# Attention item 0 ahead of two modulation steps, S5's angles six tiles later, constants behind the opening's last row

## The reference

```
proj = (h @ w_in).astype(f32)
m_qk, m_v, m_o, m_i, m_f, s_u, n_q, n_kv, n_g = jnp.split(proj, offs, axis=-1)
y_m = mlstm_group(...)      # 4 heads of 128, chunked over 128 tokens
y_s = s5_group(s_u, ...)    # complex diagonal state space, 32 groups of 16 channels, 64 states
y_n = nsa_group(...)        # 8 query heads, compressed, selected and windowed attention
```

## Time and profile before

| | |
|---|---|
| median of 3 runs | 2417.62 us (2417.16 to 2422.07) |
| profiled execution | 2417.42 us, its span 2415.5 us, granted clock 0.993 |
| TensorE busy | 2348.9 us, 97% |
| VectorE busy | 1861.1 us, 77% |
| ScalarE busy | 1291.3 us, 53% |
| GpSimd busy | 227.4 us, 9% |
| chain that ended last | PE 78%, DVE 14%, DMA 3%, ACT 3%, issue 2% |
| read from memory | 626.68 MB, 266 GB/s over the span |

### The profile page before, as it was taken

The page is one execution under the profiler, slowest core; times in us unless marked ns, Lnnn a source line. Parts: engine busy times, 40 slices in busy tenths (PEclk is TensorE's granted clock), DMA queues, the critical chain, the costliest instruction groups (busy, mean ns, idle before and its releaser), DMA issues.

```text
span 2415.5 us, 40088 instructions
## 1 busy us (share of the span) xinstructions
PE 2348.9 (97%) x13932; PEld 2053.2 (85%) x13932; DVE 1861.1 (77%) x2739; ACT 1291.3 (53%) x2164; POOL 227.4 (9%) x384
## 2 busy tenths in 40 slices
PE   6899999999999999999999999999999999999998
PEld 4689988788888888888889999877888888888887
DVE  7989998879999999666679987567896666665555
ACT  5365665555545545444468757655554554554444
POOL 1111111101111111000001130000110000000000
PEclk8999999999999999999999999999999999999999
DMA  9999788859999999788856865456795555555554
GB/s 379 403 391 346 276 284 304 322 196 347 341 350 341 342 341 343 238 293 271 279 205 219 312 249 169 172 184 254 296 331 191 187 187 190 189 187 205 195 193 146
DMA packets 189211, 643.06 MB, mean 266 GB/s; under 512 B 19089, under 2 KB 41809, under 8 KB 183329
## 3 DMA queue, kind: packets, MB, share of 16 engines
q1 hardware_dynamic: 125346, 421.72, 48.4%
q0 software_dynamic: 51264, 205.04, 24.1%
q10 hardware_dynamic: 12480, 14.72, 1.7%
HBM read 626.68 MB, written 14.71 MB: 266 GB/s over the span
## 4 chain that ended last, share of the span: by engine, by line
PE 78%; DVE 14%; DMA 3%; ACT 3%; issue 2%; POOL 0%; ACTq 0%; DVEq 0%; POOLq 0%
PE ps L1381 25%; PE ps L850 18%; PE ps L1389 13%; PE ps L833 9%; PE ps L1278 4%; DVE w_lo L2050 3%; DVE ada_w L2056 3%; DVE mix L2050 2%; DMA ada_w<-ada_d 2%; PE ps L818 2%; DMA ada_lo<-ada_d 1%; DVE side L2050 1%; ACT w_hi L1462 1%; PE ps L1292 1%; DVE mix L2056 1%
## 5 line engine op out<-in xcount | busy, mean ns | idle before, releaser
L2050 DVE TENSOR_TENSOR w_lo<-ring,w_hi 128x1024 fp32r<-128x1024 f32 x708 | 869.2, 1233 | 424.8 <-ACT w_hi L1462 421.1
L1462 ACT ACTIVATE w_hi<-ring 128x1024 fp32r<-128x1024 f32 x708 | 750.0, 1060 | 776.9 <-PE ps L850 244.9
L1381 PE MATMUL ps<-hT,w_hi 128*128 128x512 f32 x2688 | 642.2, 391 | 0.0
L1381 PEld LDWEIGHTS ps<-hT,w_hi 128*128 128x128 f32 x2688 | 493.9, 188 | 95.7
L2056 DVE SCALAR_TENSOR_TENSOR ada_w<-ada_w,cs_row 128x1024 f32<-128x1024 f32 (+1 forms) x332 | 406.7, 1260 | 14.5 <-DMA ada_w<-ada_d 14.2
L833 PE MATMUL ps<-hT,w_hi 128*128 128x256 f32 x2176 | 406.5, 289 | 5.5 <-DVE w_lo L2050 3.5
L833 PEld LDWEIGHTS ps<-hT,w_hi 128*128 128x128 f32 x2176 | 342.5, 193 | 16.1 <-issue 13.6
L1389 PEld LDWEIGHTS ps<-hT,w_lo 128*128 128x128 f32 x2688 | 344.6, 191 | 13.1
L1389 PE MATMUL ps<-hT,w_lo 128*128 128x256 f32 x2688 | 348.7, 283 | 0.0
L833 PE MATMUL ps<-hT,w_lo 128*128 128x256 f32 x1088 | 309.3, 284 | 0.0
L833 PEld LDWEIGHTS ps<-hT,w_lo 128*128 128x128 f32 x1088 | 210.1, 193 | 0.0
(11 more groups left out here) (327 smaller groups left out, 2356.0 us busy)
## 6 DMA issues: line engine op xcount, KB each, us to landing
ring<-stream SPq DMA_DIRECT2D x746, 512.0 KB, 4.8
ada_w<-ada_d POOLq DMA_DIRECT2D x320, 512.0 KB, 6.4
ada_w<-ada_d POOLq DMA_DIRECT2D x12, 1024.0 KB, 12.7
ada_lo<-ada_d POOLq DMA_DIRECT2D x10, 1024.0 KB, 15.7
ada_hi<-ada_d POOLq DMA_DIRECT2D x10, 1024.0 KB, 13.2
mix<-stream SPq DMA_DIRECT2D x14, 512.0 KB, 14.1
xs<-x SPq DMA_DIRECT2D x2, 2048.0 KB, 10.5
s_in_w<-mix ACTq DMA_DIRECT2D x8, 512.0 KB, 6.7
```

What stands on the lines that cost most here:

```text
L1381: m = pe.matmul(ps[:, bank, :], w_hi[:, (c + half) % SPLIT, kk * P:(kk + 1) * P], hT[:, k, :, :], start=k == 0, stop=k == KT - 1)
L1462: s.activation(w_hi[:, c % SPLIT, :], ring[:, at % RING, :], ACT.Copy).then_inc(hi_ready, 1)
L2050: return v.tensor_tensor(o, a, b, op)
```

## The change

Three edits. In layer 0 two modulation steps go from tile 26 to tiles 36 and 37, and at tile 27 the step that stood before `weighted(0)` stands behind it. The rest of the constants is loaded behind the last row of the opening, and TensorE waits for it before its first whole mixer tile. In layer 1 `s5_phases` is at tile 14 instead of 8, `s5_phases_cos` at 17 instead of 11, and the two sines of ScalarE at 18 instead of 12.

```diff
@@ -173,8 +173,8 @@
 U_DOWN, N_DOWN = (18, None), (2, 0)
 
 
-ADA_TILE = ({11: 3, 12: 3, 13: 3, 14: 1, 15: 1, 16: 1, 17: 2, 18: 2, 19: 2, 20: 2, 21: 2, 22: 1, 23: 2, 24: 1, 25: 1, 26: 3,
-             27: 2, 28: 3, 29: 1, 30: 3, 31: 3, 32: 3, 33: 6, 34: 4, 35: 5, 36: 4, 37: 3, 38: 2, 39: 3},
+ADA_TILE = ({11: 3, 12: 3, 13: 3, 14: 1, 15: 1, 16: 1, 17: 2, 18: 2, 19: 2, 20: 2, 21: 2, 22: 1, 23: 2, 24: 1, 25: 1, 26: 1,
+             27: 2, 28: 3, 29: 1, 30: 3, 31: 3, 32: 3, 33: 6, 34: 4, 35: 5, 36: 5, 37: 4, 38: 2, 39: 3},
             {0: 2, 15: 1, 16: 1, 18: 2, 19: 1, 26: 4, 28: 1, 32: 1, 33: 3})
 ADA_PIECE = ([1] * 24, [0] * 6 + [1] * 16)
 
@@ -722,8 +722,7 @@
                 pool.dma_start(head_slot(n), ada_rows[head_group(n), :, :]).then_inc(head_full[n % HEAD_SLOTS], 16)
                 if n == 1:
                     pool.dma_start(aux[:, GAINS:], aux_d[0, :, GAINS:]).then_inc(aux_in, 16)
-                if n == HEAD_SLOTS - 1:
-                    pool.dma_start(cst[:, K_FIRST:], consts[:, K_FIRST:]).then_inc(cst_rest, 16)
+            pool.dma_start(cst[:, K_FIRST:], consts[:, K_FIRST:]).then_inc(cst_rest, 16)
             for l in range(DEPTH):
                 rc = rope_c[:, :].unsqueeze(1).to_broadcast([P, 2, SEQ])
                 rs = rope_s[:, :].unsqueeze(1).to_broadcast([P, 2, SEQ])
@@ -925,7 +924,6 @@
 
                 def s5_b_transposes():
 
-                    pe.wait_ge(cst_rest, 16)
                     pe.wait_ge(aux_in, l * 16 + 16)
                     for part, name in ((0, "s_b_re"), (1, "s_b_im")):
                         for ut in range(UT):
@@ -1190,6 +1188,7 @@
                         if k in HEAD_OWN:
                             s5_own_weights(HEAD_OWN.index(k))
                     s5_in_weights(len(HEAD_IN))
+                    pe.wait_ge(cst_rest, 16)
                 for n in range(0 if l else HT, NT):
                     if l == 0 and n < HT + 2:
                         in_ev.wait(pe, l, 2 * (n - HT) + 2)
@@ -1868,7 +1867,7 @@
                             own_weights(len(HEAD_OWN) + LATE_C.index(n - 3))
                     if 0 <= n - BLOCKS_AT[l] < 2:
                         blocks(n - BLOCKS_AT[l])
-                    if n == (S5_B[1] + 3 if l else HT + 6):
+                    if n == (S5_B[3] + 3 if l else HT + 6):
                         tables(0)
                         tables(1)
                     for i in range(2):
@@ -2551,7 +2550,8 @@
                         glu_z.wait(v, l, 4)
                         glu_y.by(tt(mix[:, T_U:T_U + 4, :], mix[:, T_U:T_U + 4, :], glu_z_t, ALU.mult))
                     if 0 <= k - ITEM_TILE < NI:
-                        mixer_ada(min(ada_share(l, k - 1) + (2 if k in (GT_SLOT, GT_SLOT + 2) else 1), ada_share(l, k)))
+                        if k > ITEM_TILE:
+                            mixer_ada(min(ada_share(l, k - 1) + (2 if k in (GT_SLOT, GT_SLOT + 2) else 1), ada_share(l, k)))
                         weighted(k - ITEM_TILE)
                     mixer_ada(ada_share(l, k))
                     if l:
@@ -2571,9 +2571,9 @@
                             s5_weights_c(S5_B.index(k - 1))
                     elif k in LATE_C:
                         s5_weights_c(len(HEAD_OWN) + LATE_C.index(k))
-                    if k == (S5_B[0] + 2 if l else HT + 4):
+                    if k == (S5_B[2] + 2 if l else HT + 4):
                         s5_phases()
-                    if k == (S5_B[1] + 2 if l else HT + 5):
+                    if k == (S5_B[3] + 2 if l else HT + 5):
                         s5_phases_cos()
                     if k == ITEM_TILE + 2:
                         gate_chain()
```

## The result

The changed kernel takes 2421.72 us in the median of 22 runs (2417.64 to 2429.98), the kernel before 2419.01 us in the median of as many (2416.93 to 2422.07). The ratio over all these runs (it is not that of the two medians) is 1.0014, 95% interval 1.0008 to 1.0021: slower by 0.14%, under the 0.2% at which I would have called it slower, and not the 0.2% faster that I forecast. Its runs also scatter more upward: six of the 22 lie from 2427.07 to 2429.98 us. The profiled execution took 2419.80 us (span 2418.0).

A forecast was written before the change was run, and what follows sets the result against it. TensorE, busy 97% of the span, with VectorE as the bound from 259 us until 323.62. The terms +0.1 - 1.1 - 4.1 = -5.1 us took 2417.42 to 2412.3 us, range 2408.8 to 2418.2.

The forecast's parts named there:

- Part C: Layer 1, S5's phases, cosines and sines moved later: wait at tile 11 and half clock behind it go, -4.1 us.
- the step that failed: ScalarE near 1384 us: sines in front of a w_hi that TensorE needs some 8 us later; 0.2 us for small slips.
- The steps of C before it: Layer 1: tile 11 gains 4.3 us, phases take 3.75 us, tile 17's w_lo is ready with 2 us slack.
- GpSimd's next rotary multiplication: Before at 1350 to 1355 us: phases cheap or dear by whether it has ended; drawn out again, 3.15 us more.
- Rival (3): Slower: wait over 2.5 us at tile 17 or 18 plus half clock, 4.3 us; 2420.4 us, chance 0.14 with other losses.
- Part A: Layer 0, modulation steps moved from ahead of attention item 0 to tiles 36 and 37: +0.1 us in all.
- The first half: Attention item 0: TensorE's 2.83 us wait and half clock go, but VectorE bounds, so 2.29 us gained at 370 us.
- The term "+0.1 us" for the whole: Layer 0 modulation steps: 2.29 us gained, then paid back by item 11; bounds -2.3 and +4.1 us.
- the price of the two added steps: Tiles 36 and 37: 1.14 us each plus 0.2 us waiting for a chunk, taking -2.29 to +0.1 us.
- come two steps later in the same slots: Tiles 31 to 35: steps waiting for chunks move along with the relief, so 2.29 us gain remains at 370 us.
- Part B: Opening, constants behind the last modulation row: opening ends 1.7 us sooner, 0.6 us given back, -1.1 us.
- for a loss the moved bytes would have to cost more later: Opening's constants: no loss expected because DMA engines were full there; bounds -1.7 and 0 us.

The follow-up runs named there:

- sine_split: Changed kernel with the first of ScalarE's two sines moved from tile 18 to 17 in layer 1; 2423.59 us, ratio 1.0020 to the kernel before.
- nine: Kernel before with only S5's phases in layer 1 moved, from tile 8 to tile 9; 2418.42 us, ratio 0.9998.
- c_alone: Kernel before with only the layer 1 edit: phases at tile 14, cosines at 17, sines at 18; 2421.36 us, ratio 1.0012.
- a_late: Kernel before with only the modulation-step edit, its two added steps at tiles 38 and 39 instead of 36 and 37; 2420.73 us, ratio 1.0008.
- split_steps: Changed kernel with one sine at tile 17 instead of 18 and tile 18's two modulation steps at tile 21; 2415.74 us, ratio 0.9987 to the kernel before.
- a_alone: Kernel before with only the modulation-step edit of layer 0, including the step behind weighted(0); 2420.97 us, ratio 1.0010.
- bc_fixed: Kernel before with the constants edit and the layer 1 edit, one sine at tile 17, tile 18's modulation steps at 21; 2413.70 us, ratio 0.9989.
- steps_later: Changed kernel with tile 18's two modulation steps of layer 1 at tile 21, both sines still at 18; 2427.64 us, ratio 1.0035 to the kernel before.
- b_alone: Kernel before with only the constants loaded behind the opening's last row and TensorE's wait for them moved; 2419.48 us, ratio 1.0012.
- after: The changed kernel itself, all three edits against the kernel before; median 2421.72 us, ratio 1.0014, profiled execution 2419.80 us.
- c_fixed: Kernel before with only the layer 1 edit, one sine at tile 17 and tile 18's two modulation steps at 21; 2414.57 us, ratio 0.9984.
- b_look1: b_alone unchanged, profiled once more; 2416.57 us, first full mixer tile at 146.9 us.

## Why the prediction was wrong

**Part C, the step that failed.** "ScalarE loses one table load, 1.28 us, and has the two sines now in front of a `w_hi` near 1384; TensorE needs that chunk some 8 us later [...]" TensorE does not need the chunk at once, but VectorE's queue does (it came at 1388.82, not 1384): behind that `w_lo` stands S5's scan, and TensorE waits for the scan to have read its accumulators, not for the weights. Before the change this had 0.87 us of slack, and TensorE was to come 3 to 4 us sooner. With it the step cost 5.9 us, the wait of 2.55 and the half clock behind it, where the prediction had 0. I named what is queued behind the waiting instruction on ScalarE, and stopped there. The steps of C before it were right: 4.1 us at tile 11, `w_lo` of tile 17 in time, the phases at 3.75 us.

**The second chain.** I weighed GpSimd's next rotary multiplication only against the phases. The cosines at tile 17 stand in front of the modulation steps of tile 18, their chunk issues on POOL and the rotary multiplications behind them, and kept all of these at their old times; part C does not move one instruction on POOL's queue. The rule that I cited from the Trainium skill, "SBUF — State Buffer", section "Who interferes with whom" (an exclusive lock for a whole instruction) fits `sine_split`, with two `w_lo` in 5.9 us, and `nine`, with four in 6.8 us. GpSimd's third multiplication there fits it too: it takes 2.17 us, to 1.2 us behind the end of the first `w_lo`, where one that meets nothing takes 1.30.

**Rival (3) named the direction and nearly the size, not the place.** It has a wait of over 2.5 us at tile 17 or 18 and a fallen clock, 4.3 us. It came between tiles 20 and 21: 5.9 us in the changed kernel, 7.1 in `c_alone`. Its condition, a slip of tile 17's `w_lo`, did not occur.

**Part A.** The first half was right: TensorE is 2.3 us sooner at item 4, the wait at item 0 is gone, and the half clock behind it too, in this execution. (Of the six traces with that wait gone, `a_late` and `split_steps` have a half clock of 3.4 us some 10 us further on, behind a wait of 0.7 to 0.8 us.) The term "+0.1 us" for the whole was +1.0 in `a_alone` and +1.4 in the changed kernel, and more beside traces without A, which make up 0.2 to 1.0 us between 275 and 400 us by themselves: against `c_alone` it is 1.9 us in `a_alone`. Mis-sized was first the price of the two added steps. TensorE loses 3.3 us from 379 to 397 us in `a_alone` and 3.0 in the changed kernel, where the sum has 2.4 (from -2.29 to +0.1); of the difference 0.5 us is the chunk of tile 36, waited for 0.65 to 0.73 us instead of 0.2. The sentence that all chunks "come two steps later in the same slots" held in some executions alone: just ahead of item 10 the gain was 2.3 us in `a_alone` and 2.8 in `a_late`, but 1.6 in the changed kernel, whose wait for a chunk at 346.72 had grown from 2.33 to 3.50 us. Up to tile 36 these three have the same order in this part, so that this growth belongs to the change is not shown.

**Part B.** -1.1 us was forecast; at 275 us, ahead of part A, TensorE is 0.4 to 1.5 us ahead in four of the six traces in which the opening went its usual way, and 0.6 and 0.7 us behind in the other two (`bc_fixed`, with a half clock at 206 us, and `steps_later`). The median of `b_alone` shows no gain. What I had excluded ("for a loss the moved bytes would have to cost more later") happens by another way: in part of the executions the opening ends 5 to 7 us later than before. That two queues pace each other there was in the trace, as waits of POOL for chunks of SP's, and I used only the mean rate.

**The sum.** With the terms of the two traces: A +1.4, B -1.5, C -4.1 + 5.9 = +1.8, and +1.0 for the half clock at 1247: +2.7 us, near the +2.5 us at which the traces end. The terms are read from the same traces, so this shows that none is missing, not that each would be the same in another execution. The forecast had -5.1; C accounts for 5.9 us of the difference. The 95% interval of the ratio, +1.9 to +5.1 us, holds the sum; B's late openings come on top. Taken by themselves the three parts measured +0.10, +0.12 and +0.12%, together 0.34%, where the whole has 0.14%. With intervals of 0.09% on either side of each, no run shows whether the parts don't add or the numbers scatter. The profile that I added to, 2417.42 us, also lay 1.6 us under the median of the 22 runs.

Left open: why B's opening goes one of two ways (no run changed the order of SP's and POOL's transfers against each other), why the clock falls behind the same wait in one execution and not in another, and how much of A's extra waits is the place and how much the landing time of single chunks.

## What to carry to other kernels

When work is moved onto a queue, follow the queue behind it to its end on each engine: the instruction that is delayed may be needed late, and the one behind it at once. Slack that the move needs should be read as the smallest gap in the stretch between the operation that frees or fills a buffer and the one that waits for it, here 0.87 us. Where two chains end within a microsecond of each other, taking away one shows nothing; try both before either is called innocent. And when a median moves against the profile, look at the single runs: two groups ask for a profile of each.

## What was not expected of the hardware

- A GpSimd multiplication over 128x512 (1.30 us when it meets no VectorE operation) costs the VectorE operations beside it about as much again: a `w_lo` of 1.14 us took 2.32 us beside one and 3.68 us beside two (`sine_split`). The multiplication itself takes up to 2.3 us when the VectorE operation is ahead of it.
- Every new wait of TensorE of 1.9 us or more in the mixers (`after`, `c_alone`, `sine_split`, `steps_later`, `nine`) was followed by a stretch at the lower clock, 3.4 to 10.2 us long, and its length differed between executions of nearly the same wait. Beyond the wait itself TensorE lost 1.5 us by it in `nine`, 3.3 us in three of the others and 4.7 us in `c_alone`.
- An old wait is not always followed by one. TensorE waits 2.0 us near 1246 us in all 14 traces (L796 of the kernel before), and the clock fell behind it in six. It waits 2.6 to 2.8 us at item 0 in the eight traces without part A; the clock fell in six of them, for 6.8 us in the kernel before and for 3.4 in five, and not at all in `c_fixed` and `b_look1`. So my reading of the earlier trace rows, that a wait of this length brings the lower clock with it, was taken from one execution.
- At 206 us the clock fell in five traces, of kernels with and without each part, for a loss of 2.0 to 2.3 us (4.9 in `nine`); near 1247 us it cost 0.8 to 1.5 us. Traces differ by that much without an edit nearby.
